# First stage of a two-layer trunk: squares of x taken as it lies and summed on TensorE, tiles 0 and 1 in halves, unread products ahead of the data

## The chip, the cores and the metric

The kernel runs on one core of a Trainium2 chip. The metric is the device time of one execution in microseconds (us), as the median of several runs. Engines: TensorE (PE, with its weight loads as PEld), VectorE (DVE), ScalarE (ACT), GpSimd (POOL), and SyncE (SP), which here only issues DMAs.

## What is computed

Two residual layers over x of 512 tokens by 1024 features, float32. The part that the change touches is the norm of the first layer and the first projections behind it:

```python
def rmsnorm(x, g):
    x32 = x.astype(jnp.float32)
    y = x32 * lax.rsqrt(jnp.mean(x32 * x32, axis=-1, keepdims=True) + NORM_EPS)
    return (y * g.astype(jnp.float32)).astype(x.dtype)

def reference(...):
    h = x
    for layer in range(DEPTH):              # DEPTH = 2
        u = rmsnorm(h, norm_g[layer])
        ...                                 # layer 0: dsa_mixer, layer 1: dilated_mixer
        h = h + y

def dsa_mixer(h, w_in, w_out):
    q, k, v, iq, ik, iw, z = _split(h @ w_in, A_SPLITS)
    q, k = rotary(...), rotary(...)
    iq, ik = rotary(...), rotary(...)
    ...                                     # indexer scores, top 128 keys, attention, gate, w_out
```

## The kernel before

**Layout.** x and everything after it lie turned: features on the 128 partitions (8 blocks, the tile `h`), 512 tokens along the free axis. A projection is cut in tiles of 128 output features. Each weight tile is one DMA of 512 KB into `w_raw` (two buffers, tile g into g % 2) and is split in a high part `w_hi` (ScalarE, rounded to fp32r) and a low part `w_lo` (the difference; GpSimd in `split_w`, VectorE in `split_early` for tiles 0 and 1). `u` = x times the gain is split likewise: `u_hi` on ScalarE, `u_lo` on VectorE. Each of the 8 feature blocks of a tile is then three products on PE (high by high, high by low, low by high), in the order `M_ORDER`.

**The norm of the first layer.** The projections start from x times gain, unnormed; the factor rstd of each token is multiplied in behind PE. The factor comes in these steps: `square_rows` on ScalarE squares x, loaded a second time with tokens on the partitions (`x_rows`, four DMAs of 512 KB into `gated`), and sums along the row; `root` takes the square root of the four columns of sums; VectorE takes the reciprocal and writes four diagonal blocks (`diagonal`); PE multiplies ones by them, which spreads the 512 factors over all partitions (`spread`, a plain float32 matmul of 512 columns); VectorE copies that to `rstd`, multiplies it into `rotated` and two tables, and goes on with the rope of the index queries (`index_rope`, `by_sin`, `by_cos`), which also reads the PSUM bank that a later tile needs.

**The order on PE.** Written out by hand: tile `G_IK` (0, all 512 tokens) and `G_IQ[0]` (1, 384 tokens, called CHOOSING) interleaved by halves; `G_IQ[1]` (2); the turning of `iw` (three small transposes); five of the eight steps of `G_IQ[2]` (3); the spread; the other three steps; `G_Z[0]` (4); `G_V` (5), which waits for its PSUM bank to be read by `by_cos`; then the index scores. Every engine has its own program and they meet at semaphores. All later parts (the heads, the output projections, layer 1) follow in a fixed order and are not touched.

## Time and profile before

| | |
|---|---|
| median of 3 runs | 953.39 us (950.73 to 954.07) |
| profiled execution, its time | 953.82 us |
| profiled execution, its span | 952.0 us |
| PE busy | 931.0 us, 98% of the span |
| DVE, POOL, ACT busy | 64%, 59%, 44% |
| read from HBM | 78.52 MB |

The span runs from the first instruction to the last; the time has what lies around it as well. A row of the timeline says when an instruction (or a merged group of them) starts, how long it takes, its engine and line, what it writes and reads, and in brackets how long its engine stood idle just before and what ended that. Matmuls are pipelined, so the time of one is longer than the distance to the next; the distance is what a matmul costs.

### The profile page before, as it was taken

What the parts mean: (1) busy time and instruction counts of PE and PEld (TensorE: products, weight loads), DVE (VectorE), ACT (ScalarE), POOL (GpSimd) and SP (SyncE); (2) the same over time, 40 slices, a digit from 0 to 9 for tenths busy, and PEclk for the clock granted to TensorE, in tenths of its full rate; (3) what the DMA queues carried; (4) which work ended last, traced back from release to release, by engine and by line L of the source; (5) the groups of instructions that cost most, each with busy time, mean ns of one, the idle gap of its engine ahead of it and who ended that gap; (6) DMA issues with size and microseconds to landing.
All of it is one profiled execution on the core that took longest, in us unless ns stands there. A gap on an engine that the chain in (4) does not pass through costs nothing.

```text
span 952.0 us, 13321 instructions
## 1 busy us (share of the span) xinstructions
PE 931.0 (98%) x4931; PEld 804.1 (84%) x4931; DVE 613.7 (64%) x1246; ACT 423.4 (44%) x772; POOL 564.3 (59%) x395
## 2 busy tenths in 40 slices
PE   6899999999999999999999999999999999999996
PEld 6798788888888888888888898989898888988886
DVE  4899698766656641138766666676777666665126
ACT  5664422455545543243443445452543434453323
POOL 2775544455555544447666776667766667764435
PEclk9999999999999999999999999999999999999998
DMA  8421323111111123222222212222222222122312
GB/s 293 158 96 67 104 96 102 54 45 45 66 46 45 46 87 111 89 66 67 89 90 89 89 67 67 89 89 76 81 67 89 90 89 88 60 96 89 111 44 89
DMA packets 25136, 81.48 MB, mean 86 GB/s; under 512 B 2928, under 2 KB 5232, under 8 KB 25072
## 3 DMA queue, kind: packets, MB, share of 16 engines
q1 hardware_dynamic: 23920, 79.57, 25.5%
q10 hardware_dynamic: 1152, 1.06, 0.3%
q8 instruction: 39, 0.64, 0.3%
q14 instruction: 25, 0.20, 0.1%
HBM read 78.52 MB, written 2.10 MB: 85 GB/s over the span
## 4 chain that ended last, share of the span: by engine, by line
PE 90%; DVE 4%; POOL 3%; issue 2%; ACT 1%; DMA 0%; POOLq 0%; ACTq 0%; DVEq 0%
PE ps L323 16%; PE ps L325 15%; PE ps L324 15%; PE ps L460 6%; PE ps L458 6%; PE ps L459 6%; PE ps L356 3%; PE ps L357 3%; PE ps L358 3%; PE ps L404 2%; PE ps L405 2%; PE ps L403 2%; PE ps L418 2%; POOL square_sum L1303 1%; PE ps L439 1%
## 5 line engine op out<-in xcount | busy, mean ns | idle before, releaser
L1295 POOL TENSOR_TENSOR w_lo<-w_raw,w_hi 128x1024 fp32r<-128x1024 f32 x137 | 338.8, 2479 | 180.9 <-ACT w_hi L641 179.3
L323 PE MATMUL ps<-u_hi,w_hi 128*128 128x512 f32 (+1 forms) x728 | 285.0, 391 | 11.0 <-DVE u_lo L946 8.3
L325 PE MATMUL ps<-u_hi,w_lo 128*128 128x512 f32 (+1 forms) x728 | 281.2, 386 | 0.0
L324 PE MATMUL ps<-u_lo,w_hi 128*128 128x512 f32 (+1 forms) x728 | 280.9, 386 | 0.0
L323 PEld LDWEIGHTS ps<-u_hi,w_hi 128*128 128x128 f32 x728 | 137.4, 189 | 37.2 <-issue 7.5
L325 PEld LDWEIGHTS ps<-u_hi,w_lo 128*128 128x128 f32 x728 | 137.1, 188 | 26.3
L324 PEld LDWEIGHTS ps<-u_lo,w_hi 128*128 128x128 f32 x728 | 137.4, 189 | 24.8 <-issue 0.2
L641 ACT ACTIVATE w_hi<-w_raw 128x1024 fp32r<-128x1024 f32 x138 | 143.7, 1053 | 26.4 <-DMA w_raw<-weights 21.5
L1083 DVE STREAM_TRANSPOSE bias_a<-probs 32x320 f32<-32x320 f32 x240 | 120.7, 503 | 18.4 <-POOL probs L1338 15.3
L1338 POOL TENSOR_SCALAR probs<-probs,inv_den 128x512 f32<-128x512 f32 (+3 forms) x128 | 66.2, 537 | 88.6 <-DVE inv_den L1072 88.6
L734 ACT ACTIVATE probs<-neg_s,neg_max 128x512 f32<-128x512 f32 (+3 forms) x128 | 70.6, 553 | 57.4 <-DVE neg_max L1065 57.1
L1346 POOL TENSOR_TENSOR pT_lo<-bias_a,pT_hi 128x768 fp32r<-128x768 f32 (+1 forms) x30 | 53.6, 1806 | 67.7 <-ACT pT_hi L748 67.7
L748 ACT ACTIVATE pT_hi<-bias_a 128x768 fp32r<-128x768 f32 (+1 forms) x30 | 20.5, 731 | 120.4 <-DVE bias_a L1083 120.4
L356 PE MATMUL ps<-w_hi,u_hi 128*128 128x256 f32 x256 | 72.9, 285 | 0.5 <-POOL w_lo L1295 0.5
L357 PE MATMUL ps<-w_lo,u_hi 128*128 128x256 f32 x256 | 72.4, 283 | 0.0
L358 PE MATMUL ps<-w_hi,u_lo 128*128 128x256 f32 x256 | 72.4, 283 | 0.0
L1003 DVE TENSOR_TENSOR by_sin<-ps,scaled 64x512 f32<-64x512 f32 x96 | 66.1, 688 | 3.9 <-PE ps L325 0.7
L1090 DVE TENSOR_TENSOR pT_lo<-ps,pT_hi 128x384 fp32r<-128x384 f32 (+1 forms) x51 | 27.5, 595 | 53.1 <-ACT pT_hi L740 53.1
L1115 DVE TENSOR_TENSOR gated<-ps,gated 128x512 f32<-128x512 f32 x32 | 22.1, 690 | 49.7 <-PE ps L440 41.4
L460 PE MATMUL ps<-o_hi,w_lo 128*128 128x512 f32 x128 | 50.4, 394 | 0.0
L356 PEld LDWEIGHTS ps<-w_hi,u_hi 128*128 128x128 f32 x256 | 49.1, 192 | 1.4 <-POOL w_lo L1295 0.9
L459 PE MATMUL ps<-o_lo,w_hi 128*128 128x512 f32 x128 | 50.1, 391 | 0.0
(171 smaller groups left out, 1725.4 us busy)
## 6 DMA issues: line engine op xcount, KB each, us to landing
w_raw<-weights SPq DMA_DIRECT2D x138, 512.0 KB, 3.3
gated<-x_rows SPq DMA_DIRECT2D x4, 512.0 KB, 7.6
h<-x_turned SPq DMA_DIRECT2D x7, 256.0 KB, 6.5
outT<-h SPq DMA_DIRECT2D x10, 128.0 KB, 2.0
outT<-h ACTq DMA_DIRECT2D x6, 128.0 KB, 2.2
w_raw<-weights SPq DMA_DIRECT2D x2, 256.0 KB, 5.1
table<-rope_tables SPq DMA_DIRECT2D x2, 256.0 KB, 6.9
table<-rope_tables SPq DMA_DIRECT2D x1, 512.0 KB, 8.5
```

What stands on the lines that cost most here:

```text
L323: pe.matmul(out, w_hi[:, g % SLOTS, blk], u_hi[:, k, tokens], start=(at == 0), stop=False)
L324: pe.matmul(out, w_hi[:, g % SLOTS, blk], u_lo[:, k, tokens], start=False, stop=False)
L325: last = pe.matmul(out, w_lo[:, g % SLOTS, blk], u_hi[:, k, tokens], start=False, stop=(at == KT - 1))
L356: pe.matmul(out, u_hi[:, k, tokens], high, start=(j % 2 == 0 and at == 0), stop=False)
L357: pe.matmul(out, u_hi[:, k, tokens], low, start=False, stop=False)
L358: last = pe.matmul(out, u_lo[:, k, tokens], high, start=False, stop=(j % 2 == 1 and at == KT - 1))
L459: pe.matmul(out, w_hi[:, g % SLOTS, blk], lo[:, tokens], start=False, stop=False)
L460: return pe.matmul(out, w_lo[:, g % SLOTS, blk], hi[:, tokens], start=False, stop=final)
L641: act.activation(w_hi[:, g % SLOTS, :], w_raw[:, g % 2, :], ACT.Copy).then_inc(w_hi_ready, 1)
L734: act.activation(probs[:, cols], neg_s[:, cols], ACT.Exp, bias=neg_max[:, i:i + 1], scale=-1.0, accum_out=den[:, i:i + 1]).then_inc(exp_do ...
L1083: last = dve.transpose(target[cols_at:cols_at + 32, :, rows_at:rows_at + 32], source[rows_at:rows_at + 32, :, cols_at:cols_at + 32])
L1295: pool.tensor_tensor(w_lo[:, g % SLOTS, :], w_raw[:, g % 2, :], w_hi[:, g % SLOTS, :].bitcast(F32), ALU.subtract).then_inc(w_lo_ready, 1)
```

## The change

x is no longer loaded a second time as rows. ScalarE squares the eight blocks of `h` as they lie (`first_square`), and PE sums the squares over the partitions with 32 matmuls of one column (`sum_first_squares`: 8 blocks by 4 groups of 128 tokens), behind tile `G_IQ[1]`. Tiles 0 and 1 are loaded and split in halves. Tile 2 is loaded into `neg_s`, which is idle then, without waiting for a buffer, and split by ScalarE and VectorE. PE starts with 11 products of ones by ones that nobody reads, and the first tiles' products come in another order: `high_step` (which needs no `u_lo`) ahead of `low_step`.

```diff
+WARM, WARM_BANK = 11, 7
...
+        third_raw = neg_s[:, 0:D_MODEL]
...
-            sp.dma_start(w_raw[:, 0, 0:half], weights[0][:, 0:half]).then_inc(first_half_landed, 16)
-            for m in (1, 2, 3):
-                sp.dma_start(h[:, m, :], xT[m * P:(m + 1) * P, :]).then_inc(x_landed[m], 16)
-            load_tile(1)
-            sp.dma_start(w_raw[:, 0, half:], weights[0][:, half:]).then_inc(w_landed[0], 16)
+            load_half(0, one, halves_landed[0])
+            load_x(1)
+            load_half(1, one, halves_landed[1])
+            load_x(2)
+            load_x(3)
+            load_half(0, other, w_landed[0])
+            load_half(1, other, w_landed[1])
             for m in (4, 6, 7, 5):
-                sp.dma_start(h[:, m, :], xT[m * P:(m + 1) * P, :]).then_inc(x_landed[m], 16)
-            load_tile(2)
+                load_x(m)
+            sp.dma_start(third_raw, weights[2]).then_inc(third_landed, 16)
             load_tile(3)
...
-            for i in range(QB):
-                load_rows(i)
...
+            def sum_first_squares():
+                for at in range(KT):
+                    pe.wait_ge(first_squares_ready, at + 1)
+                    for i in range(QB):
+                        last = pe.matmul(ps[:, S_BANK, i:i + 1], square[:, at, i * P:(i + 1) * P], ones[:, 0:1],
+                                         start=(at == 0 and i == 0), stop=(at == KT - 1 and i == QB - 1))
+                last.then_inc(first_sums_done, 1)
...
+            def high_step(g, at, tokens, hi, lo):
+
+                k = M_ORDER[at]
+                blk = slice(k * P, (k + 1) * P)
+                out = ps[:, BANK[n_of(g)], tokens]
+                pe.wait_ge(w_hi_ready, hi)
+                pe.matmul(out, w_hi[:, g % SLOTS, blk], u_hi[:, k, tokens], start=(at == 0), stop=False)
+                pe.wait_ge(early_lo_ready, lo)
+                pe.matmul(out, w_lo[:, g % SLOTS, blk], u_hi[:, k, tokens], start=False, stop=False)
...
             pe.wait_ge(ones_ready, 1)
-            pe.wait_ge(early_lo_ready, 1)
-            for at in range(KT // 2):
+            for _ in range(WARM):
+                pe.matmul(ps[:, WARM_BANK, 0:P], ones[:, :], ones[:, :], start=True, stop=True)
+
+            for at in range(2):
+                pe.wait_ge(u_hi_ready, at + 1)
+                high_step(G_IK, at, ALL, 1, 1)
                 pe.wait_ge(u_lo_ready, at + 1)
-                step(G_IK, at)
...
+                low_step(G_IK, at, ALL)
+            for at in range(2):
+                high_step(G_IQ[0], at, CHOOSING, 2, 2)
+                low_step(G_IQ[0], at, CHOOSING)
+            for at in range(2, KT):
+                pe.wait_ge(u_hi_ready, at + 1)
+                late = 2 if at >= KT // 2 else 0
+                high_step(G_IK, at, ALL, 1 + late, 1 + late)
+                high_step(G_IQ[0], at, CHOOSING, 2 + late, 2 + late)
                 pe.wait_ge(u_lo_ready, at + 1)
-                step(G_IK, at)
-                step(G_IQ[0], at, CHOOSING)
+                low_step(G_IK, at, ALL)
+                low_step(G_IQ[0], at, CHOOSING)
             project(G_IQ[1], tokens=CHOOSING)
+            sum_first_squares()
             turn_iw()
-            project(G_IQ[2], range(0, 5), tokens=CHOOSING)
+            project(G_IQ[2], range(0, 3), tokens=CHOOSING)
             spread(S_BANK, QB)
-            project(G_IQ[2], range(5, KT), tokens=CHOOSING)
+            project(G_IQ[2], range(3, KT), tokens=CHOOSING)
...
             for m in (4, 6, 7, 5):
-                act.wait_ge(x_landed[m], 16)
-                split_u(0, m)
-            split_w(2)
+                first_u(m)
+            first_square(0)
+            act.wait_ge(third_landed, 16)
+            act.activation(w_hi[:, 2, :], third_raw, ACT.Copy).then_inc(w_hi_ready, 1)
+            for at in range(1, 5):
+                first_square(at)
             split_w(3)
-            for i in range(QB):
-                square_rows(i)
+            for at in range(5, KT):
+                first_square(at)
             act.wait_ge(eps_ready, 1)
-            act.wait_ge(rows_summed, QB)
-            root(root_turned[:, :], row_sums[:, :])
+            act.wait_ge(first_sums_done, 1)
+            root(root_turned[:, :], ps[:, S_BANK, 0:QB])
...
+            split_early(2, slice(0, D_MODEL), 5, third_raw)
```

How PE's program begins. Before, tile 0 (512 columns) has its three products together from the first on:

```order
L323 MATMUL ps<-u_hi,w_hi 128x512
L324 MATMUL ps<-u_lo,w_hi 128x512
L325 MATMUL ps<-u_hi,w_lo 128x512
L323 MATMUL ps<-u_hi,w_hi 128x512
L324 MATMUL ps<-u_lo,w_hi 128x512
```

Now the products of ones stand ahead, and the product with `u_lo` is the last of each three (L593 and L595 are `high_step`, L600 is `low_step`):

```order
L608 MATMUL ps<-ones 128x128 x11
L593 MATMUL ps<-u_hi,w_hi 128x512
L595 MATMUL ps<-u_hi,w_lo 128x512
L600 MATMUL ps<-u_lo,w_hi 128x512
L593 MATMUL ps<-u_hi,w_hi 128x512
L595 MATMUL ps<-u_hi,w_lo 128x512
L600 MATMUL ps<-u_lo,w_hi 128x512
L593 MATMUL ps<-u_hi,w_hi 128x384
```

So the first product no longer stands behind a `u_lo`, and tile 1 (384 columns) comes in after two blocks of tile 0 instead of four.

PE between `G_IQ[1]` and `G_IQ[2]`. Before, the last products of `G_IQ[1]` are followed by the turning of iw (L366):

```order
L323 MATMUL ps<-u_hi,w_hi 128x384
L324 MATMUL ps<-u_lo,w_hi 128x384
L325 MATMUL ps<-u_hi,w_lo 128x384
L366 MATMUL ps<-ident,probs 128x16 x3
L323 MATMUL ps<-u_hi,w_hi 128x384
```

Now the one-column matmuls (L297, `sum_first_squares`) stand between them, and the spread (L328) comes three steps later instead of five:

```order
L335 MATMUL ps<-u_hi,w_hi 128x384
L336 MATMUL ps<-u_lo,w_hi 128x384
L337 MATMUL ps<-u_hi,w_lo 128x384
L297 MATMUL ps<-ones,gated 128x1 x32
L378 MATMUL ps<-ident,probs 128x16 x3
L335 MATMUL ps<-u_hi,w_hi 128x384
```

All of `G_IQ[2]` and the spread therefore stand behind the 32 new matmuls.

ScalarE up to the root. Before, the four squarings of rows (L675) stand between the high parts of tiles 2 and 3 (L641) and the root (L679):

```order
L644 ACTIVATE u_hi<-h,gain 128x512 x4
L641 ACTIVATE w_hi<-w_raw 128x1024 x2
L675 ACTIVATE gated,row_sums<-gated 128x1024 x4
L679 ACTIVATE root_turned<-row_sums,eps 128x4
L641 ACTIVATE w_hi<-w_raw 128x1024
```

Now the squarings of blocks of `h` (L712) stand around those high parts, and the root (L715) reads PSUM:

```order
L682 ACTIVATE u_hi<-h,gain 128x512 x4
L712 ACTIVATE gated<-h 128x512
L875 ACTIVATE w_hi<-neg_s 128x1024
L712 ACTIVATE gated<-h 128x512 x4
L679 ACTIVATE w_hi<-w_raw 128x1024
L712 ACTIVATE gated<-h 128x512 x3
L715 ACTIVATE root_turned<-ps,eps 128x4
L679 ACTIVATE w_hi<-w_raw 128x1024
```

The root now waits for PE's sums instead of ScalarE's own.

## Rows read from the trace of the kernel before

**Rows 1.** The page, busy time by engine.

```profile
PE 931.0 (98%) x4931; PEld 804.1 (84%) x4931; DVE 613.7 (64%) x1246; ACT 423.4 (44%) x772; POOL 564.3 (59%) x395
```

**Rows 2.** Waits, 0 to 70 us: total, times, longest.

```profile
PE ps L323 <- DVE by_cos L1019: 2.6, 2, 2.2
```

**Rows 3.** Timeline of PE at the start.

```profile
7.28 0.76 PE L323 MATMUL ps<-u_hi,w_hi 128*128 128x512 f32 x1 [7.28 <-DVE u_lo L946]
...
7.84 0.63 PE L324 MATMUL ps<-u_lo,w_hi 128*128 128x512 f32 x1
...
8.27 0.63 PE L325 MATMUL ps<-u_hi,w_lo 128*128 128x512 f32 x1
...
11.68 0.44 PE L324 MATMUL ps<-u_lo,w_hi 128*128 128x512 f32 x1
...
11.96 0.40 PE L325 MATMUL ps<-u_hi,w_lo 128*128 128x512 f32 x1
...
12.19 0.34 PE L323 MATMUL ps<-u_hi,w_hi 128*128 128x384 f32 x1
```

**Rows 4.** Timeline of PE, 19 to 38 us: `G_IQ[1]`, turning, spread, `G_V`.

```profile
19.23 0.44 PE L323 MATMUL ps<-u_hi,w_hi 128*128 128x384 f32 x1
...
23.59 0.35 PE L366 MATMUL ps<-ident,probs 16*128 16x16 f32 x3
23.88 0.45 PE L323 MATMUL ps<-u_hi,w_hi 128*128 128x384 f32 x1
...
26.70 1.13 PE L316 MATMUL ps<-square_sum,ones 128*128 128x512 f32 x2
...
34.83 0.39 PE L325 MATMUL ps<-u_hi,w_lo 128*128 128x512 f32 x1
37.40 0.50 PE L323 MATMUL ps<-u_hi,w_hi 128*128 128x512 f32 x1 [2.18 <-DVE by_cos L1019]
...
37.97 0.40 PE L325 MATMUL ps<-u_hi,w_lo 128*128 128x512 f32 x1
```

**Rows 5.** Timeline of ScalarE, 5 to 26 us.

```profile
5.54 2.62 ACT L644 ACTIVATE u_hi<-h,gain 128x512 fp32r<-128x512 f32 x4 [0.36 <-DMA gain<-gains]
...
10.23 2.55 ACT L644 ACTIVATE u_hi<-h,gain 128x512 fp32r<-128x512 f32 x4
...
20.13 1.06 ACT L675 ACTIVATE gated<-gated 128x1024 f32<-128x1024 f32 x1 [2.20 <-DMA gated<-x_rows]
...
25.22 0.30 ACT L679 ACTIVATE root_turned<-row_sums,eps 128x4 f32<-128x4 f32 x1
```

**Rows 6.** Timeline of VectorE, 11 to 38 us.

```profile
11.59 2.73 DVE L946 SCALAR_TENSOR_TENSOR u_lo<-h,gain,u_hi 128x512 fp32r<-128x512 f32 x4
...
25.76 0.88 DVE L963 TENSOR_SCALAR square_sum<-ident,inv_turned 128x128 f32<-128x128 f32 x4
...
29.90 4.59 DVE L1195 TENSOR_TENSOR table<-table,rstd 128x512 f32<-128x512 f32 x2
...
36.79 0.56 DVE L1019 TENSOR_TENSOR by_cos<-ps,table 128x384 f32<-128x384 f32 x1
```

**Rows 7.** Timeline of the DMA queue of SyncE.

```profile
11.70 0.80 SPq L244 DMA_DIRECT2D w_raw<-weights  x2
```

**Rows 8.** Timeline of PE in the last norm, one-column matmuls.

```profile
942.12 0.95 PE L302 MATMUL ps<-ones,gated 128*128 128x1 f32 x8
942.93 0.58 PE L302 MATMUL ps<-ones,square_sum 128*128 128x1 f32 x4
```

**Rows 9.** Busy time in stretches: stretch, length, PE, PEld, DVE, ACT, POOL, PEclk, DMA, GB/s.

```profile
942.00:943.00 1.00, 1.00 (x11) 0.97 (x9) 0.68 (x2) 1.00 (x3) 0.29 (x2) 1.00 0.00 0
...
943.50:944.00 0.50, 0.01 (x1) 0.00 (x0) 0.18 (x2) 0.27 (x2) 0.50 (x2) 0.61 0.07 16
944.00:944.50 0.50, 0.00 (x0) 0.00 (x0) 0.47 (x3) 0.00 (x0) 0.50 (x2) 0.50 0.80 260
```

**Rows 10.** Timeline of GpSimd, 27 to 32 us.

```profile
27.04 5.20 POOL L1295 TENSOR_TENSOR w_lo<-w_raw,w_hi 128x1024 fp32r<-128x1024 f32 x2 [5.50 <-ACT w_hi L641]
```

More of the change, by code:

```diff
@@ L178, in build @@
         x_landed = [sem(f"x_landed{m}") for m in range(KT)]
-        rows_landed = [sem(f"rows_landed{i}") for i in range(QB)]
         gain_landed, bias_landed = sem("gain_landed"), sem("bias_landed")
@@ new lines, in low_step @@
+            def low_step(g, at, tokens):
+                k = M_ORDER[at]
+                blk = slice(k * P, (k + 1) * P)
+                last = pe.matmul(ps[:, BANK[n_of(g)], tokens], w_hi[:, g % SLOTS, blk], u_lo[:, k, tokens],
+                                 start=False, stop=(at == KT - 1))
+                if at == KT - 1:
+                    last.then_inc(tile_done, 1)
+            pe.wait_ge(ones_ready, 1)
+            for _ in range(WARM):
+                pe.matmul(ps[:, WARM_BANK, 0:P], ones[:, :], ones[:, :], start=True, stop=True)
@@ new lines, in _ @@
+            act.dma_start(h[:, 0, :], xT[0:P, :]).then_inc(x_landed[0], 16)
+            act.preload_act_table(ACT.Sqrt)
+            split_half(0, one, halves_landed[0])
+            act.wait_ge(gain_landed, 16)
+            first_u(0)
+            first_u(1)
+            split_half(1, one, halves_landed[1])
+            first_u(2)
+            first_u(3)
+            split_half(0, other, w_landed[0])
+            split_half(1, other, w_landed[1])
+            for m in (4, 6, 7, 5):
+                first_u(m)
```

83 lines of the change are left out of this document (37 added, 46 removed).

## Prediction

> **What bounds the kernel now.** I read the page first: TensorE (PE) is busy for 98% of the span [rows 1], so a microsecond put on PE or taken from it counts in full, unless PE then stands waiting for someone. Next the waits of the first 70 us, since the change touches nothing later: the only ones of PE that matter behind its start are 2.6 us in two waits, both for VectorE's `by_cos` [rows 2], the longer one 2.2 us. The reader is to see two things in the timelines. At the start PE does nothing until 7.28, and then its products of 512 columns follow each other at 0.43 us (7.84 to 8.27); from 11.68 they come at 0.28 and then 0.23 us [rows 3]. Those are the two levels of its clock, 1.2 and 2.4 GHz, though the page's clock column shows nothing of it: 4.4 us at the lower level. Later, PE reaches the product of tile `G_V` at about 35.1 (34.83 and 0.23) and starts it at 37.40 [rows 4]. That start is set by a chain: ScalarE's root of the row sums at 25.22 [rows 5], the diagonal on VectorE at 25.76, PE's spread at 26.70 [rows 4], the copy, three scalings, the first index rope and its `by_cos`, which ends at 37.35 [rows 6]. So the price of the change can be read at one place: when does `G_V` start, 37.40 before? Behind it the same instructions follow in the same order on every engine, and I let everything move with it.
>
> **The start of PE.** Before, the first product waits for `u_lo` (7.28). Now it waits for `u_hi` alone; the first of four began on ScalarE at 5.54 and the four took 2.62 [rows 5], so it is there at about 6.2 and PE starts at 6.3. The order of the two DMAs on ScalarE's queue (gain, then x) only swaps which of them is last. Ahead of it stand 11 unread products of 128 columns in full float32. The nearest row is the spread, 512 columns in float32: 1.13 us for its two records [rows 4], of which some 0.16 is the tail that the next instruction overlaps (a product of 384 columns lasts 0.34 at a distance of 0.18). That is 0.97, or 0.24 per 128 columns at the upper level and 0.48 at the lower. Eleven are 5.3 us, from 1.0 (the ones are written then) to 6.3, just ahead of the data. If their weight loads are not hidden as in the spread, up to twice that: PE would start at up to 10 and 4 us would be lost, which I keep for the upper end. If 4.4 us of them lift the clock as 4.4 us of products did [rows 3], the products then run at the upper level from the first. The gap of about a microsecond or less to the first product should not undo it: PE idled 2.2 us ahead of 37.40, and the product at 37.97 lasted 0.40 us as at the upper level, not 0.63 as at the lower [rows 3, 4].
>
> **The first two tiles.** 24 products of 512 columns at 0.23 and 24 of 384 at 0.18 (tile `G_IQ[1]` runs 24 in 4.36 us, 19.23 to 23.59 [rows 4]) are 9.8 us. Started at 6.3 that is 16.1. I add 0.5 for the two places where PE meets a half tile or a `u_lo` that isn't there yet: 16.6. The feeders allow it: ScalarE ran its last four `u_hi` from 10.23 without a pause to 12.8 [rows 5], VectorE its last four `u_lo` from 11.59 to 14.3 [rows 6], and both have the same amount of work to do here, only in halves; x is behind the same bytes as before. Tile 2 was asked for at 11.70, when a buffer came free [rows 7]; now it goes to `neg_s` right behind x, and VectorE makes its low part (two halves of 0.6 us) by about 16. So `G_IQ[1]` starts at 16.6 instead of 19.23, **2.6 us earlier**, and ends at 16.6 + 4.3 = 20.9 (before, 23.59).
>
> **The sums.** Removed are four DMAs of 512 KB and four squarings of 128x1024 on ScalarE, which began at 20.13 after a wait for the rows and held the root back to 25.22 [rows 5]. Added are eight squarings of 128x512 on ScalarE, about 0.65 each; these lie beside PE's products and are done by about 20, with the high parts of tiles 2 and 3 between them. They hide under PE's work. What doesn't hide is new on PE: 32 matmuls of one column, in the block behind `G_IQ[1]`. The nearest rows are the same form in the last norm: eight records from 942.12 to 942.93, 0.81 us [rows 8]; a float32 matmul leaves two records (the spread shows it), so that is 0.20 us a matmul and **6.5 us** for 32. Each loads 128 columns of weights to stream one. The Trainium skill (TensorE: Matmul & The Clock Gate, "Wait — 56ns, not 53.3ns?") says that however few columns a matmul has, starts are never closer than about 25 ns; by that floor alone 64 records would be 1.6 us. The trace has 0.10 us a record, four times the floor, so the row decides and the floor isn't what binds. With the clock as it is, the sums end at 20.9 + 6.5 = 27.4 and the root starts at 27.5: 2.3 us later than before, though PE came 2.6 us earlier.
>
> **What the sums do to the clock.** The other place in this trace where PE runs one-column matmuls for over a microsecond is the end. There the granted clock is 1.00 from 942 to 943, 0.61 in the half microsecond from 943.5, and 0.50 behind that [rows 9]: it fell from 2.4 to 1.2 GHz after 1.2 us of one-column matmuls (942.12 to 943.3) and 0.3 us of nothing. Yet 2.2 us of plain idling ahead of 37.40, with full products on both sides, did not lower it. So these matmuls look to the clock much like no work, and here come 6.5 us of them in a block. The Trainium skill (same page, "What's actually happening") says that a gate sets the clock by how busy PE has recently been; it doesn't say what one-column matmuls count as, and if they count as busy the sum is that of the first rival below. I take it that the clock falls inside the block. When is unknown: 1.5 us in (as at the end) or as late as 6.5; I take the middle, 4.0. The remaining 2.5 us then take 5.0, and the sums end at 20.9 + 4.0 + 5.0 = 29.9.
>
> **From there to `G_V`.** PE has the turning of iw (0.29, 23.59 to 23.88), three steps of `G_IQ[2]` (1.56), then what it did from 26.70 to 35.06 (8.36) and the two steps more that now stand behind the spread (1.04): 11.25 us. At the lower level for up to 4.4 us, as at the start, it loses half of that; I take 3.4 us and 1.7. PE reaches `G_V` at 29.9 + 11.25 + 1.7 = 42.9. VectorE's chain is beside that: the spread starts at 29.9 + 0.3 + 3.1 = 33.3 and 10.7 us later (26.70 to 37.40) is 44.0. But of those 10.7 a part was waiting for GpSimd: the two table scalings took 4.59 us for a piece of work that takes 0.7 each elsewhere on VectorE (its `u_lo` of the same size) [rows 6], while GpSimd split two tiles from 27.04 to 32.2 [rows 10]. GpSimd's splits follow the root, the scalings now come later behind it, and I reckon with some 3 us less. So PE's 42.9 holds. **Sum: 42.9 - 37.40 = 5.5 us slower.** The profiled execution has a span of 952.0 and a time of 953.82, so 957.5 and 959.3; the median of the runs was 953.39, 0.43 under the profiled one, so 958.9.
>
> **Bounds.** Low for this case: the clock falls at the very end of the block and is back after 2 us: 27.4 + 11.25 + 1.0 = 39.7, +2.3, median 955.7. High: it falls after 1.5 us (sums end at 32.4) and stays down for 4.4: 32.4 + 11.25 + 2.2 = 45.9, +8.5, 961.9. Unhidden weight loads of the unread products would come on top, but are the less likely, as loads overlap products everywhere in this trace.
>
> **The rivals.**
> *The clock holds* (0.22). The sums end at 27.4; the diagonal is ready 1.5 after the root at 27.5, at 29.0; PE gets to the spread at 29.3. The chain gives 40.0, PE alone 38.7. That is +1.3 to +2.6: 955.3, no difference that a measurement can tell. For it: six or seven microseconds of PE records without a gap look busy, and the fall at the end had idle time on both sides. Against it: the 2.2 us of idle time that did nothing.
> *The sums are cheap* (0.04), the one on the faster side: if one-column matmuls in a row ran at a quarter of the row's price, 1.6 us, the root would start at 22.6 and `G_V` at about 34: 3.4 us faster, 950.0. It becomes faster than before at all when 32 matmuls take under about 4.2 us. Against it stands 0.81 us for four, measured. Even sums for nothing give `G_V` no earlier than 20.9 + 11.25 = 32.2, 5 us faster, so over 0.5% is nearly out of reach.
> *The warm-up misfires* (0.06): the unread products don't lift the clock or run past 6.3. Then 2 to 4 us of the early gain go, on top of the forecast: 962.
> The forecast's own case, a fall in the block, has 0.68.
>
> **How the numbers follow.** 0.5% of 953.39 is 4.8 us, about what a measurement of this kernel can tell from no change. The forecast's case passes that in two of three of its placements (0.45), the misfire nearly always (0.05). The rest of both, the clock that holds and most of the cheap sums are within it (0.47). A gain beyond it gets 0.03, for a much shorter wait behind the sums than any row shows. The range goes from inside the holding clock's case, 954.5, to the forecast's high end, 961.9.
>
> **What would show it.** The unread products from 1.0 to about 6; the first product of `G_IK` at 6.3 and 0.23 us to the next; `G_IQ[1]` from about 16.6 to 21; the one-column block at least 6.5 us long, with 0.10 us a record at first and 0.20 behind a fall of the granted clock to 0.50; the root at about 30; `G_V` at about 43, with no wait of PE for `by_cos` ahead of it. If the clock column shows 1.00 throughout, the forecast is wrong by the clock's step; if the block is much under 6 us, by the price of a matmul; if `G_IQ[1]` starts later than 17.5, by the feeding of the first tiles.

## Result, and the profile after

The changed kernel takes **960.55 us** (median of six runs, 959.30 to 964.42). The kernel before, run beside it, takes 952.37 us (950.73 to 954.07). The ratio is 1.0085 with a 95% interval of 1.0069 to 1.0100: 0.85% slower, which is beyond what such a measurement can fail to tell from no change. The profiled execution has a span of 959.6 us and a time of 961.42; 959.6 against 952.0 is the 7.6 us that the traces have to account for. Executions of one kernel differ: the kernel before took from 950.7 to 954.1 us here, and the profiled execution of the changed kernel is the second longest of its six. So every span below is that of one execution, to be read with its own trace; whether one kernel is faster than another is told by the ratios. One execution of the later kernel e4_rows_back took 1320.81 us at a mean granted clock of 0.654 and is left out of its ratio.

The page of the changed kernel, its span, its busy times, and the row of TensorE's clock over 40 slices of the span:

```profile
span 959.6 us, 13498 instructions
...
PE 947.6 (99%) x5017; PEld 820.7 (86%) x5017; DVE 610.1 (64%) x1248; ACT 423.8 (44%) x773; POOL 561.5 (59%) x394
...
PEclk9799999999999999999999999999999999999998
```

PE is busy for 947.6 us where it was 931.0 [rows 1]: 16.6 us more. 7.6 of these are the longer span, 6.2 the idle start up to 7.28 [rows 3], which is now filled from 1.05 on, and 2.6 the two waits for `by_cos` [rows 2], which are gone. The second digit of PEclk, a 7, is a slice in which the clock was down for part of the time.

The timeline of PE in the first 45 us (start, duration, engine, line, operation, and in brackets the idle time before):

```profile
1.05 5.06 PE L608 MATMUL ps<-ones 128*128 128x128 f32 x22 [1.05 <-DVE ones L1211]
5.84 0.72 PE L593 MATMUL ps<-u_hi,w_hi 128*128 128x512 f32 x1
6.40 0.40 PE L595 MATMUL ps<-u_hi,w_lo 128*128 128x512 f32 x1
...
16.39 0.34 PE L335 MATMUL ps<-u_hi,w_hi 128*128 128x384 f32 x1
...
20.39 0.34 PE L337 MATMUL ps<-u_hi,w_lo 128*128 128x384 f32 x1
20.56 11.05 PE L297 MATMUL ps<-ones,gated 128*128 128x1 f32 x64
31.55 0.50 PE L378 MATMUL ps<-ident,probs 16*128 16x16 f32 x3
...
35.02 1.91 PE L328 MATMUL ps<-square_sum,ones 128*128 128x512 f32 x2
...
44.98 0.39 PE L335 MATMUL ps<-u_hi,w_hi 128*128 128x512 f32 x1
```

`G_IQ[1]` starts at 16.39 instead of 19.23 and its products end at 20.56 instead of 23.59 [rows 4]: PE is 3.0 us ahead. Then come the 64 records of the 32 one-column matmuls, 11.05 us without a gap, and the turning of iw starts at 31.55, 8.0 us behind its place before. `G_V` starts at 44.98, 7.6 us behind 37.40, and has no bracket: PE no longer waits for `by_cos` there.

The same stretch in windows (stretch, length, then busy time and count of PE, PEld, DVE, ACT, POOL, then PEclk, DMA share, GB/s):

```profile
20.50:23.00 2.50, 2.50 (x25) 2.50 (x23) 0.00 (x0) 0.00 (x0) 0.00 (x0) 1.00 0.78 264
23.50:31.50 8.00, 8.00 (x39) 8.00 (x38) 0.00 (x0) 0.00 (x0) 0.00 (x0) 0.50 0.15 57
31.50:36.50 5.00, 5.00 (x16) 4.14 (x16) 1.05 (x5) 3.55 (x4) 3.50 (x2) 0.50 0.07 7
37.00:39.00 2.00, 2.00 (x13) 2.00 (x13) 1.97 (x4) 0.59 (x1) 0.73 (x1) 0.98 0.65 242
```

In the first row PE has 25 records in 2.5 us at a clock of 1.00, two of which are still products of `G_IQ[1]`. The trace starts the second one-column record 0.03 us behind the first, and each further one 0.112 us behind the one before it. In the second row PE has 39 records in 8.0 us at 0.50, and they start 0.213 us apart. That distance sets in at 23.4, so there the clock fell to 1.2 GHz, after 2.8 us of one-column matmuls that filled PE entirely (the busy column is full in both rows, and the clock fell all the same). It came back only at about 37.1, 5.5 us behind the block, and every product between runs at the lower level too. The other three engines do nothing at all in the first two rows: everybody waits for the sums.

What VectorE, GpSimd and ScalarE do behind them, from their timelines:

```profile
17.24 1.67 ACT L712 ACTIVATE gated<-h 128x512 f32<-128x512 f32 x3
31.71 0.26 ACT L715 ACTIVATE root_turned<-ps,eps 128x4 f32<-128x4 f32 x1 [12.80 <-PE ps L297]
33.00 4.72 POOL L1348 TENSOR_TENSOR w_lo<-w_raw,w_hi 128x1024 fp32r<-128x1024 f32 x2 [13.11 <-ACT w_hi L679]
36.97 0.69 DVE L1243 COPY rstd<-ps 128x512 f32<-128x512 f32 x1 [3.87 <-PE ps L328]
38.30 1.28 DVE L1248 TENSOR_TENSOR table<-table,rstd 128x512 f32<-128x512 f32 x2
```

ScalarE has its squares by 18.9, 1.7 us before PE starts summing them: they hide. The root starts at 31.71, not 25.22 [rows 5]. The two table scalings take 1.28 us instead of 4.59 [rows 6]; GpSimd's split now ends at 37.7, before them. In the first trace GpSimd is busy for 4.38 of the 4.60 us in which they run, here for none of 1.30.

**Behind `G_V`** the delay isn't constant. Here are the first product of the first index score and the first product of the sixth, in the trace before:

```profile
43.11 0.48 PE L385 MATMUL ps<-ik,q_hi 128*128 128x512 f32 x1
...
76.18 0.40 PE L385 MATMUL ps<-ik,q_hi 128*128 128x512 f32 x1
```

and after:

```profile
50.42 0.39 PE L397 MATMUL ps<-ik,q_hi 128*128 128x512 f32 x1
...
81.79 0.39 PE L397 MATMUL ps<-ik,q_hi 128*128 128x512 f32 x1
```

The delay is 7.31 at the first and 5.61 at the sixth: about 2 us are given back since `G_V`. Twenty microseconds of this part as windows (columns as above), first before, then after:

```profile
46.00:66.00 20.00, 20.00 (x112) 18.75 (x113) 19.72 (x34) 14.18 (x31) 15.68 (x12) 1.00 0.34 107
52.00:72.00 20.00, 20.00 (x117) 19.45 (x116) 18.08 (x33) 14.54 (x32) 15.70 (x12) 1.00 0.32 106
```

Before, VectorE was busy for 19.72 of the 20 us; after, it is busy for 18.08, and PE gets 117 records done where it got 112. I read this as VectorE setting the pace of this part before: it gained the 3.3 us of the scalings and is now ahead of PE. Then 2.0 us are lost again further on: 0.5 in the heads of layer 0 (from the last index score to the first product on `o_hi`) and 0.76 in the output projection of each of the two layers. All products on `o_hi` and `o_lo` with the high part of the weights in one layer, grouped by line (count, then busy us and mean ns of one); first the trace before, 339 to 424 us:

```profile
L458 PE MATMUL ps<-o_hi,w_hi 128*128 128x512 f32 x64 | 25.0, 390 | 0.0
L459 PE MATMUL ps<-o_lo,w_hi 128*128 128x512 f32 x64 | 25.0, 391 | 0.0
```

then the trace after, 345 to 430 us:

```profile
L470 PE MATMUL ps<-o_hi,w_hi 128*128 128x512 f32 x64 | 25.3, 396 | 0.0
L471 PE MATMUL ps<-o_lo,w_hi 128*128 128x512 f32 x64 | 25.3, 395 | 0.0
```

The instructions are the same, no line of theirs was changed, and the clock is 1.00 in both. The duration of a product is longer than its distance to the next, so what this costs is read from the starts: from the first to the last product on `o_hi` in this layer it is 76.9 us before (340.0 to 417.0) and 77.7 after (346.2 to 423.9). +7.6 at `G_V`, 2.0 back, 2.0 lost: +7.6 at the end.

### The profile page after: what moved, and what is told of

The parts are those of the page before. It is cut to its first block, busy times and chain, and to the rows that moved or that the text cites. A ratio compares the mean times of both kernels' runs of the same rounds, so it can differ in the third digit from the quotient of the medians.

```text
span 959.6 us, 13498 instructions
## 1 busy us (share of the span) xinstructions
PE 947.6 (99%) x5017; PEld 820.7 (86%) x5017; DVE 610.1 (64%) x1248; ACT 423.8 (44%) x773; POOL 561.5 (59%) x394
## 4 chain that ended last, share of the span: by engine, by line
PE 92%; POOL 3%; DVE 3%; issue 1%; ACT 1%; POOLq 0%; DVEq 0%
PE ps L335 16%; PE ps L337 15%; PE ps L336 15%; PE ps L470 6%; PE ps L472 6%; PE ps L471 6%; PE ps L368 3%; PE ps L370 3%; PE ps L369 3%; PE ps L416 2%; PE ps L417 2%; PE ps L415 2%; PE ps L430 2%; POOL square_sum L1356 1%; PE ps L297 1%
## 5 line engine op out<-in xcount | busy, mean ns | idle before, releaser
L335 PE MATMUL ps<-u_hi,w_hi 128*128 128x512 f32 (+1 forms) x712 | 279.5, 393 | 1.0 <-DVE u_lo L993 1.0
L337 PE MATMUL ps<-u_hi,w_lo 128*128 128x512 f32 (+1 forms) x712 | 275.2, 386 | 0.0
L336 PE MATMUL ps<-u_lo,w_hi 128*128 128x512 f32 (+1 forms) x712 | 274.8, 386 | 0.0
L337 PEld LDWEIGHTS ps<-u_hi,w_lo 128*128 128x128 f32 x712 | 134.1, 188 | 26.4
L335 PEld LDWEIGHTS ps<-u_hi,w_hi 128*128 128x128 f32 x712 | 134.4, 189 | 25.9 <-DVE u_lo L993 1.4
L336 PEld LDWEIGHTS ps<-u_lo,w_hi 128*128 128x128 f32 x712 | 134.5, 189 | 24.6 <-issue 0.5
L679 ACT ACTIVATE w_hi<-w_raw 128x1024 fp32r<-128x1024 f32 x136 | 141.6, 1052 | 20.8 <-DMA w_raw<-weights 15.8
L470 PE MATMUL ps<-o_hi,w_hi 128*128 128x512 f32 x128 | 50.7, 396 | 0.0
```

The lines of the kernel that those rows point to most:

```text
L335: pe.matmul(out, w_hi[:, g % SLOTS, blk], u_hi[:, k, tokens], start=(at == 0), stop=False)
L336: pe.matmul(out, w_hi[:, g % SLOTS, blk], u_lo[:, k, tokens], start=False, stop=False)
L337: last = pe.matmul(out, w_lo[:, g % SLOTS, blk], u_hi[:, k, tokens], start=False, stop=(at == KT - 1))
L470: pe.matmul(out, w_hi[:, g % SLOTS, blk], hi[:, tokens], start=first, stop=False)
L679: act.activation(w_hi[:, g % SLOTS, :], w_raw[:, g % 2, :], ACT.Copy).then_inc(w_hi_ready, 1)
```

## The experiments

Twelve kernels; "before" is the first kernel run beside each on the same chip. The spans are those of the profiled executions and compare with 952.0.

| run | edit | median us (before) | ratio, 95% interval | span | `G_V` starts |
|---|---|---|---|---|---|
| before | | 952.37 | | 952.0 | 37.40 |
| changed kernel | | 960.55 (952.37) | 1.0085, 1.0069 to 1.0100 | 959.6 | 44.98 |
| e1_woven | sums between the steps | 963.18 (953.23) | 1.0096, 1.0081 to 1.0111 | 961.4 | 46.72 |
| e2_wide | 128 columns a sum | 958.17 (953.23) | 1.0053, 1.0036 to 1.0069 | 956.4 | 39.87 |
| e3_four_sums | 28 of 32 sums left out | 951.98 (953.23) | 0.9990, 0.9980 to 0.9999 | 950.1 | 33.48 |
| e4_rows_back | rows of x again | 953.41 (953.23) | 0.9993, 0.9982 to 1.0005 | 951.2 | 36.76 |
| e5_pad | spare tile | 958.81 (952.57) | 1.0053, 1.0037 to 1.0070 | 957.7 | 45.35 |
| e6_no_warm | no unread products | 962.42 (952.57) | 1.0099, 1.0075 to 1.0123 | 959.0 | 44.64 |
| e7_adds_pad | VectorE adds, four sums | 953.28 (952.57) | 0.9998, 0.9988 to 1.0009 | 951.1 | 36.48 |
| e8_adds_late_split | e7, one split later | 953.76 (952.57) | 1.0010, 0.9998 to 1.0021 | 951.7 | 34.12 |
| e9_adds_swap | e8, two orders swapped | 954.60 (953.59) | 1.0017, 1.0005 to 1.0028 | 953.5 | 35.47 |
| e10_before_swap | before with e9's orders | 954.06 (953.59) | 1.0004, 0.9995 to 1.0013 | 952.2 | 34.74 |
| e11_before_shift | before, `row_sums` last | 954.97 (953.59) | 1.0014, 1.0003 to 1.0025 | 953.2 | 36.78 |
| e12_wide_pad | e2 and e5 | 956.44 (953.21) | 1.0040, 1.0027 to 1.0053 | 954.3 | 39.87 |

**e1_woven: the sums between full products.** Is it the block that lowers the clock, or the narrow matmuls?

```diff
-            project(G_IQ[1], tokens=CHOOSING)
-            sum_first_squares()
+            for k in range(KT):
+                project(G_IQ[1], range(k, k + 1), tokens=CHOOSING)
+                sum_first_squares(range(k, k + 1))
```

> The 32 one-column matmuls stand four at a time behind each of the eight steps of tile G_IQ[1] instead of in one block; nothing else differs from the changed kernel. If the block lowers the clock (theory), products between them keep it at the upper level: the granted clock shows 1.00 from about 6 us on, the 64 records cost 6.4 us (0.10 each), G_IQ[1] and the sums together take 16.4 to 27.2, and G_V starts between 38.5 and 39.5 instead of 44.98: about 955 us, 5.5 to 6.5 faster than the changed kernel, 1 to 2 slower than before. If the matmuls are dear in themselves and the clock's fall is a bystander (rival), the place makes no difference: about 11 us for them, G_V near 45, 960.5.

The clock fell all the same, earlier (at 21.7) and for longer (to 38.8). Two of the eight groups in PE's timeline, one on either side of the fall, and the window behind it:

```profile
19.93 0.95 PE L297 MATMUL ps<-ones,gated 128*128 128x1 f32 x8
...
26.34 1.70 PE L297 MATMUL ps<-ones,gated 128*128 128x1 f32 x8
```

```profile
23.50:31.50 8.00, 8.00 (x35) 8.00 (x34) 0.00 (x0) 0.00 (x0) 0.00 (x0) 0.50 0.16 62
```

Eight records take 0.95 us at first and 1.70 behind the fall, though each group has 0.5 us of 384-column products ahead of it. So it isn't the unbroken block; my expectation missed, and this order costs 1.8 us of span more than the block does.

**e2_wide: the same sums with 128 columns.** Each matmul streams all of `ones` instead of its first column, and the root reads every 128th column of the bank.

```diff
-                        last = pe.matmul(ps[:, S_BANK, i:i + 1], square[:, at, i * P:(i + 1) * P], ones[:, 0:1],
+                        last = pe.matmul(ps[:, S_BANK, i * P:(i + 1) * P], square[:, at, i * P:(i + 1) * P], ones[:, :],
...
-            root(root_turned[:, :], ps[:, S_BANK, 0:QB])
+            root(root_turned[:, :], ps[:, S_BANK, 0:SEQ:P])
```

> The block stays where it is, with the same 32 weight loads, but each matmul streams 128 columns of ones instead of one (the sum then stands in 128 equal columns, and the root reads one of them). If the clock falls because the block streams one column at a time (theory), it holds now at 1.00; a record costs the longer of load and stream, about 0.107 us, so the block takes 6.8 us, 20.6 to 27.4, and G_V starts at 38.7 to 39.7: about 955.5 us although 128 times as many columns are streamed. If the clock fell because of the many weight loads or the small size of the instructions (rival), it falls here too and the block takes 11 us or more: 960.5 or slower.

The timeline of PE and, for the stretch in question, the window:

```profile
20.77 7.31 PE L297 MATMUL ps<-ones,gated 128*128 128x128 f32 x64
28.01 0.35 PE L378 MATMUL ps<-ident,probs 16*128 16x16 f32 x3
...
39.87 0.50 PE L335 MATMUL ps<-u_hi,w_hi 128*128 128x512 f32 x1 [0.80 <-DVE by_cos L1066]
```

```profile
23.50:31.50 8.00, 8.00 (x60) 7.37 (x59) 1.53 (x6) 3.29 (x4) 2.03 (x1) 1.00 0.15 59
```

The clock stays at 1.00 throughout. 128 columns cost 0.113 us a record (7.24 us over 64, starts 0.112 apart): the same as one column in the changed kernel ahead of its fall, and a little more than I had expected. The turning starts 3.5 us sooner than in the changed kernel. This is the rival "the clock holds" made real, and `G_V` lands where that rival put it: 39.87, forecast 40.0 by VectorE's chain. The chain binds again because the scalings are back at 4.59 (32.36 to 36.95), beside GpSimd, which is busy for 4.78 of the 5.0 us from 31.5. The end, though, is 4.4 us late, not 2.5, and the median misses my 955.5: two more microseconds go behind `G_V`, and this pointed at the output projections.

**e3_four_sums: what the sums cost in all.** This kernel leaves out 28 of the 32 sums (only the last block's four remain), so its norm is taken over an eighth of the features.

```diff
+                    if at < KT - 1:
+                        continue
...
-                                         start=(at == 0 and i == 0), stop=(at == KT - 1 and i == QB - 1))
+                                         start=(at == KT - 1 and i == 0), stop=(at == KT - 1 and i == QB - 1))
```

> Leaves out 28 of the 32 one-column matmuls (only the last of the eight squared blocks is summed), so that the norm's factor is not the reference's: the price of the block, with everything else of the change in place. The four take 0.8 us, the root starts at about 21.5, the clock holds, and G_V is set by the chain of VectorE, 12.2 us behind the root, at 33.6 (PE alone would be there at 32.6): 3.8 us faster than before, 11.4 faster than the changed kernel, about 948.7. If instead the early part of the change has a cost of its own that the block hides, it stays above 952.

The root starts at 21.76 and `G_V` at 33.48, 3.9 us ahead of before; the rival of cheap sums had said about 34. The span is only 1.9 us shorter, since 2.0 are lost behind, as in e2, which my 948.7 had not reckoned with. Even nearly free sums don't bring 0.5%.

**e4_rows_back: the new start with the old norm.** The rows of x are loaded again and squared by ScalarE, the one-column matmuls are gone, and the spread is back behind five steps; halves, unread products and the order of the first tiles stay.

```diff
+            for i in range(QB):
+                sp.dma_start(rows[:, 2 * i:2 * i + 2, :], x_rows[i]).then_inc(rows_landed[i], 16)
...
-            sum_first_squares()
             turn_iw()
-            project(G_IQ[2], range(0, 3), tokens=CHOOSING)
+            project(G_IQ[2], range(0, 5), tokens=CHOOSING)
             spread(S_BANK, QB)
...
+            for i in range(QB):
+                act.wait_ge(rows_landed[i], 16)
+                act.activation(rows[:, 2 * i:2 * i + 2, :], rows[:, 2 * i:2 * i + 2, :], ACT.Square,
+                               accum_out=row_sums[:, i:i + 1]).then_inc(rows_summed, 1)
```

> The norm as before (x loaded again as rows, squared and summed on ScalarE, spread behind five steps), with the rest of the change: halves, unread products, tile 2 in neg_s. PE ends G_IQ[1] at 20.6 instead of 23.5. If the early gain of PE is swallowed by the wait for the norm (theory), the root starts only as much earlier as the rows land earlier, 0 to 2 us, the wait of PE ahead of G_V grows from 2.2 to 3.5 or more, and the time is 950.5 to 952.4. If PE's early start counts by itself (rival), it is 2.9 faster than before: 949.5 and no longer wait.

The waits in PE's timeline, at the spread and at `G_V`:

```profile
26.20 1.12 PE L335 MATMUL ps<-square_sum,ones 128*128 128x512 f32 x2 [2.24 <-DVE square_sum L1015]
...
36.76 0.50 PE L342 MATMUL ps<-u_hi,w_hi 128*128 128x512 f32 x1 [2.21 <-DVE by_cos L1071]
```

`G_IQ[1]` starts at 16.54, 2.7 us early, and PE hands all but 0.6 of it back. It does so in the first of these waits, at the spread; the second was there before, and hasn't grown as I had expected. The last of the rows' squarings still waits for its rows, the root starts at 24.73 (25.22 before), and from there the chain to `by_cos` is as long as it was. The lead of 0.6 us stays to the end, with no loss in the output projections. In the time that is nothing (0.9993). So the half of the change that feeds PE earlier works and is worth nearly nothing alone.

**e5_pad: is it where tiles lie?** The change drops the 16-byte tile `row_sums`, and every tile allocated behind it moves. This kernel puts an unused tile in its place.

```diff
+        spare = sb("spare", [P, QB])
         root_turned = sb("root_turned", [P, QB])
```

> The changed kernel with one unused tile of 16 bytes a partition where row_sums was allocated, so that every later tile in SBUF stands where it stood before the change; no instruction differs. Behind the first stage the changed kernel, the wide and the four-sums kernels all lose a further 2 us on products that read tiles allocated behind that place (heads of layer 0, both output projections), and the kernel with the rows back, which has row_sums again, loses none. If that is the place of the tiles (theory), the distance of products in the output projections falls back from 0.232 to 0.230 us and the kernel is 2.0 us faster than the changed one: 958.5. If it comes from the added instructions on PE (rival), nothing changes: 960.5.

The output projections, same view as above (345 to 430 us):

```profile
L471 PE MATMUL ps<-o_hi,w_hi 128*128 128x512 f32 x64 | 25.0, 390 | 0.0
L472 PE MATMUL ps<-o_lo,w_hi 128*128 128x512 f32 x64 | 25.0, 391 | 0.0
```

390 and 391 ns again, and the loss is gone: the seventh index score starts 5.75 us late (89.85 against 84.10, after 7.95 at `G_V`), and the end is 5.7 late. The median is 1.7 us under that of the changed kernel, and the span 1.9. In this execution the first stage went another way than in the changed kernel's: the first product came at 6.62, the clock was low until 10.6 in spite of the unread products, the sums began at 22.57 and took 9.0 us (the clock fell at 27.7). The two differences nearly cancel (turning at 31.50 and 31.55).

**e6_no_warm: without the unread products.**

```diff
-WARM, WARM_BANK = 11, 7
+WARM, WARM_BANK = 0, 7
```

> The changed kernel without the 11 unread products. If they lift the clock ahead of the data (theory), the first product still starts at 5.8, but products run at the lower level until about 10, G_IQ[1] starts 2 us later, at 18.4 instead of 16.4, and the block behind it as much: 962.5. If the clock would have been up anyway by the second or third product (rival), it starts at 16.5 and the time stays 960.5.

The first product is at 6.04, with its successors 0.42 us apart, and `G_IQ[1]` starts 1.3 us later (17.70). The block again, in PE's timeline:

```profile
21.87 9.11 PE L297 MATMUL ps<-ones,gated 128*128 128x1 f32 x64
30.91 0.50 PE L378 MATMUL ps<-ident,probs 16*128 16x16 f32 x3
```

It is 1.9 us shorter, as the clock fell at 26.9, so the turning is earlier than with the unread products. The medians (962.42 and 960.55, intervals that overlap) don't tell the two kernels apart. This kernel's executions themselves fall apart in two pairs, 960.78 and 960.88 us at a mean granted clock of 0.991, 963.96 and 964.16 at 0.989 and 0.990, so the clock doesn't behave alike in all executions of one kernel. The unread products are worth 1.3 us at `G_IQ[1]` between these two executions, nothing in e5's, and what follows swallows it.

**e7_adds_pad: fewer sums.** VectorE adds the eight squared blocks (seven additions of 128x512) and PE sums the one that remains with four matmuls, behind three steps of `G_IQ[2]`; the spread is behind six; spare tile as in e5.

```diff
             def sum_first_squares():
-                for at in range(KT):
-                    pe.wait_ge(first_squares_ready, at + 1)
...
+                pe.wait_ge(first_added, KT - 1)
...
+            def add_first(blocks):
+                for at in blocks:
+                    dve.wait_ge(first_squares_ready, at + 1)
...
+                    dve.tensor_tensor(square_sum[:, :], square[:, 0, :] if at == 1 else square_sum[:, :],
+                                      square[:, at, :], ALU.add).then_inc(first_added, 1)
```

> VectorE adds the eight squared blocks (three adds behind the low part of tile 2, four behind the products of G_IK), so that PE sums one block with 4 matmuls of one column, placed behind three steps of G_IQ[2], and the spread stands three steps later; with the unused tile of 16 bytes. The adds end at about 23.2, the root starts at 24.1, the clock holds at 1.00, and with the chain as in the kernel before (12.2 us, 3 of it waiting for GpSimd's splits) G_V starts at 36.2: 1.2 faster than before, 952. If the clock falls all the same, or the adds wait for GpSimd, it is no faster than before.

The clock stays at 1.00, as with the norm of before. The last of the additions and the wait at `G_V`, from the timelines of VectorE and PE:

```profile
20.55 3.08 DVE L1224 TENSOR_TENSOR square_sum<-square_sum,gated 128x512 f32<-128x512 f32 x4
```

```profile
36.48 0.50 PE L336 MATMUL ps<-u_hi,w_hi 128*128 128x512 f32 x1 [2.18 <-DVE by_cos L1068]
```

The additions end at 23.6, so the root starts at 24.84, where e4's did, and `G_V` is 0.9 us early. All of it stays to the end (span 951.1), and it is too little to be measured (0.9998).

**e8, e9 and e10: moving the wait.** Since the scalings are slow only beside GpSimd, e8 lets ScalarE release GpSimd's second split later.

```diff
             act.preload_act_table(ACT.Silu)
-            split_w(5)
...
             act.activation(ik[P // 2:P, 0, :], rotated[0:P // 2, 0, :], ACT.Copy).then_inc(rope_hi_ready, 1)
+            split_w(5)
             split_w(6)
```

> As the kernel with adds on VectorE, and ScalarE makes the high part of tile 5 behind the two copies to ik instead of ahead of them, so that GpSimd's split of tile 5 no longer stands beside VectorE's scaling of the tables. If the chain's 4.59 us for the two scalings is a wait for GpSimd (theory), they take 1.3, by_cos ends 8.5 to 9 us behind the root, at about 33, and G_V is set by PE at 33.3: 4 us faster than before, 949. If the scalings are slow by themselves (rival), it is as the kernel without this edit.

The scalings on VectorE, and PE's next wait:

```profile
28.99 1.28 DVE L1260 TENSOR_TENSOR table<-table,rstd 128x512 f32<-128x512 f32 x2
```

```profile
41.75 0.58 PE L398 MATMUL ps<-ik,q_hi 128*128 128x512 f32 x1 [1.93 <-POOL q_lo L1395]
```

The scalings take 1.28, `G_V` starts at 34.12 without a wait, 3.3 us ahead of before, and 1.9 of that is waited away at the first index score: GpSimd does the deferred split first and has the low part of the query late. Right behind that wait the granted clock is 0.50, from 42.0 to 45.4, and PE is only 0.5 us ahead at the second score. The end is 0.3 us ahead in span, nothing in time, where I had expected 949. e9 puts that low part ahead of the next split, and ScalarE's high part (`index_hi`) ahead of its own.

```diff
-            split_w(6, moved=R_IQ)
-            index_lo(0, 6)
-            pool.wait_ge(rope_lo_ready, R_IQ + 1)
+            pool.wait_ge(rope_lo_ready, R_IQ)
+            index_lo(0, 5)
+            split_w(6, moved=R_IQ + 1)
```

> The kernel with adds on VectorE and the late split of tile 5, and with the split of tile 6 behind the low and high parts of the first index queries instead of ahead of them, on ScalarE and on GpSimd. There the wait had moved to the first index scores (1.93 us for GpSimd's q_lo). If it was that split that held them back (theory), that wait goes, the clock doesn't fall behind it, and the time is 2.5 to 3.3 us below the kernel before: 949.5 to 950. If another wait takes its place, it stays within 1 us of the kernel before.

The waits of PE, 0 to 70 us (total, times, longest):

```profile
PE ps L398 <- DVE score L1089: 2.5, 4, 1.5
```

Now VectorE is late with the first scores; its waits have one of 3.9 us for ScalarE to have read the products. There is a second loss, ahead of `G_V` (35.47, where e8 had 34.12): the clock fell at 25.7, about a microsecond behind the four one-column sums, and was back at 29.1. In e7 and e8 the same four sums didn't lower it.

```profile
25.00:29.00 4.00, 4.00 (x12) 2.97 (x12) 1.05 (x5) 2.50 (x3) 2.35 (x1) 0.59 0.01 4
```

The kernel is 0.17% slower than before, by an interval (1.0005 to 1.0028) just clear of none, instead of the gain that I had expected. e10 makes both moves, e8's and e9's, in the kernel before, whose norm is untouched.

> The kernel before, with those two moves alone (split of tile 5 behind the copies to ik, split of tile 6 behind the first index queries), nothing of the change. The two table scalings take 1.3 us instead of 4.59 and the wait of 2.2 us ahead of G_V goes: 2 to 2.5 us faster than before, 950.5. If the gain of the other kernel needs the adds, it is the same as before.

```profile
PE ps L385 <- DVE score L1040: 2.5, 4, 1.4
```

The same wait of the same size, in another kernel: the scalings take 1.28, the wait of 2.2 at `G_V` is gone, PE is 2.9 us early at the first index score, and at the end it has nothing (952.2, ratio 1.0004). My 950.5 is missed as well. The clock holds in this trace, so it is the cleanest of the three: with VectorE busy for 19.72 of 20 us in the index scores, PE can't keep a lead into them, and to take the wait for `by_cos` away only moves it there.

**e11_before_shift: the placement alone.** In the kernel before, `row_sums` is allocated last; nothing else changes.

```diff
-        row_sums = sb("row_sums", [P, QB])
         root_turned = sb("root_turned", [P, QB])
...
         top8 = sb("top8", [P, QB - 1, 8])
+        row_sums = sb("row_sums", [P, QB])
```

> The kernel before, with the tile row_sums allocated last in SBUF instead of ahead of root_turned, so that all later tiles stand where they stand in the changed kernel; no instruction differs. If the place of the tiles costs what the pad gave back (theory), the output projections run at 0.232 us a product and the time is 1.7 to 2.0 us above the kernel before: 954.7. If not, it is the same.

The output projections once more (339 to 424 us):

```profile
L458 PE MATMUL ps<-o_hi,w_hi 128*128 128x512 f32 x64 | 25.3, 396 | 0.0
L459 PE MATMUL ps<-o_lo,w_hi 128*128 128x512 f32 x64 | 25.3, 395 | 0.0
```

396 and 395 ns: moving 16 bytes reproduces the dearer products in a kernel without any part of the change. The output projection takes 77.7 us from its first product on `o_hi` to its last, as in the changed kernel, and the heads of layer 0 take 0.5 us more, as there. Behind the first stage it loses 1.8 us; that stage ended 0.6 us early here, and the span is 953.2. The ratio, 1.0014, is clear of none (from 1.0003).

**e12_wide_pad: both repairs.** 128 columns and the spare tile.

> The two edits together that each gave back a part of the change's loss: the block streams 128 columns a matmul, and the unused tile of 16 bytes puts the later tiles in their old places. If the loss of the change is made of these two and of what PE does more (theory), what is left is the distance of G_V in the wide kernel's trace, 39.87 against 37.40: 2.5 us above the kernel before, 955 to 956, and the output projections at their old price. If the two overlap (rival), it stays where the wide kernel is, 958.

The block takes 7.2 us (20.77 to 28.00), `G_V` is at 39.87 as in e2, products on `o_hi` cost 390 ns, and the span is 954.3, +2.3: the 2.5 at `G_V` and nothing lost behind. By their ratios alone e12 and e2 can't be told apart (the intervals overlap); it is the traces that show what the spare tile gives back. Two expressions and a tile of 16 bytes take the ratio from 1.0085 to 1.0040; it is still slower than before.

## Why the prediction came out as it did

**The number came out right**, with 960.55 inside the range and the slower side forecast, and part of that is luck. The 958.9 stood on a median of 953.39 for the kernel before, which over six runs is 952.37: forecast were 5.5 us more, measured are 8.2 in the medians and 7.6 in the spans. The mechanism, a fall of the clock inside the block, is what happened.

**The price of a one-column matmul was taken a little low.** The prediction divided 0.81 us by eight records [rows 8]. But the first of the eight is followed by the second after 0.03 us, and the others are 0.112 apart there, as they are here. At full clock 64 records are 7.1 us, not 6.5 (e2 and e3 show the same distance).

**The early gain held, in this execution.** `G_IQ[1]` at 16.39 (forecast 16.6), its end at 20.56 (20.9), the first product at 5.84 (6.3). e5's execution of the same start had none of the gain from the clock, so "16.6" was one outcome among several.

**The clock fell in the block, and the term was mis-sized twice.** The prediction put the fall 4.0 us in and the sums' end at 29.9; it came 2.8 us in, the block took 11.05 us instead of 9.0, and the turning started at 31.55. About half of these 2 us is the earlier fall and half the dearer record (with the fall at 4.0, 36 records at 0.112 and 28 at 0.213 are 10.0 us). Behind the block I took 3.4 us at the lower level and 1.7 of loss; it was 5.5 us, and from 31.55 to 44.98 PE needed 13.43 us for what I had counted as 11.25: 2.2 of loss. Together 1.65 and 0.5 late: 44.98 instead of 42.9. Both lay within the bounds given (39.7 to 45.9). e2 shows that this term is the clock: the same sums, the clock at 1.00, `G_V` 5.1 us earlier.

**VectorE's relief held.** 3.3 us less for the two scalings where some 3 were reckoned, and PE alone sets `G_V`. The Trainium skill (SBUF — State Buffer, "Who interferes with whom") says that a VectorE instruction with two inputs in SBUF contends with a GpSimd instruction that reads SBUF. The traces agree: 4.59 us for the pair of scalings, which read `table` and `rstd`, with GpSimd busy for 4.38 of 4.60 us (before and e3), 1.28 with GpSimd idle throughout (changed kernel and e10).

**What the prediction had wrong** is the last sentence of its first part, that behind `G_V` the same instructions follow and everything moves along. Two things there were not seen. About 2 us came back in the index scores; my reading is that the relieved VectorE sets the pace there. In its favour, nothing comes back in e2, e3 and e12, where GpSimd's splits lie beside the scalings as before, and 2.0 to 2.3 us do in e1, e5 and e6, where they don't; no run changes the scalings alone in the changed kernel. And 2.0 us were lost because the change also moves every tile behind `row_sums`, which e5 (tile put back: 390 ns) and e11 (tile moved in the kernel before: 396 ns) show from both sides. 1.5 of the 2.0 are the two output projections and 0.5 the heads of layer 0. It is luck that the two things cancel, so that the total was off by the block and the clock behind it alone: 7.6 against 5.5 in the span.

**The rivals.** "The clock holds" didn't happen, but e2 shows its number to be sound. "The sums are cheap" gave about 34 for `G_V`, and e3, with nearly no sums, has 33.5. The number doesn't follow from the prediction's own rows, though: with sums of 1.6 us PE gets to the spread at 24.4, and 10.7 later is 35.1. "The warm-up misfires" was no case of its own: it happened in e5's execution, and the time didn't show it.

**Open.** The rows had cost PE nothing but a wait further down, and nothing I tried made sums on PE worth their price. The heads of layer 0 grow by 0.5 us in every kernel with moved tiles (the changed kernel, e1, e2, e3, e6, e11) and by nothing in e4, e7 and e12, but by 0.2 in e5 and 0.4 in e8, e9 and e10, whose tiles lie as before, and I have no cause for those. What sets the moment at which the clock falls, between 2.8 us (changed kernel) and 5.0 or 5.1 us (e6, e5) into the same block, isn't settled either. The traces show only that where the clock rose later it also fell later: it rose at 6.3 and fell at 23.4 in the changed kernel, 9.8 and 26.9 in e6, 10.6 and 27.7 in e5. So what the unread products gain at the start can be given back in the block: against e6, which has none, the changed kernel is 1.3 us ahead at `G_IQ[1]` and 0.6 us behind at the turning.

## What to carry to other kernels

On a bound TensorE, a sum over partitions by one-column matmuls is paid twice: by its count (0.11 us a record, two records each in float32) and by the clock, which drops beneath them and stays down for full products behind them. Stream 128 columns at the same price, or add on another engine first (four sums left the clock alone in e7 and e8, not in e9). When a gain arrives at the front of a chain, follow it to the next engine that has no slack before counting it: here PE's lead of 3 us was worth 0.6 to 0.9 in the span (e4, e7) and nothing that the medians show, and taking the next wait away only made another. And when a tile is removed, compare the cost of unchanged instructions far away before crediting or blaming the change.

## What the runs showed of the hardware

- TensorE can be busy without a gap, with weight loads alongside, and its clock still falls to 1.2 GHz: one-column matmuls for 2.8 us in the changed kernel, 5.1 in e5, 5.0 in e6. Full products mixed in at about a third of the time (e1) don't hold it; 128 columns instead of one do (e2, e12).
- A float32 matmul of one column and one of 128 columns, each with a weight load of 128 columns of its own, cost the same: 0.112 us from record to record at a granted clock of 1.00 (changed kernel, e2), two records a matmul. At 0.50 the one-column record costs 0.213.
- In e4 the granted clock was 0.50 from 38.2 to 41.6, behind two idle waits of 2.2 us ten microseconds apart. In e8 it was 0.50 from 42.0 to 45.4, behind a wait of 1.9 that ended at 41.75. In e9 it was 0.50 from 25.7 to 29.1, behind a wait of 0.9 and eight one-column records. In the kernel before a single wait of 2.2 did nothing to it, nor did one of 2.2 in e7 and in e11. That the waits lowered it is not shown.
- A matmul of 512 columns takes 395 or 396 ns instead of 390 or 391 when the tiles it reads lie elsewhere in SBUF, by the size of one 16-byte tile, and an output projection 77.7 us instead of 76.9, 1% more. It was measured on products with `o_hi` and `o_lo` and in both directions (e11, e5); the runs don't show which address makes the difference.
